# Another order of the weight units in the expert steps of a two-layer transformer trunk

## The reference, cut to what matters

```python
combine = jnp.sum(jax.nn.one_hot(top_idx, 8) * top_w[..., None], axis=1)
for e in range(8):
    out = out + combine[:, e:e+1] * ((silu(t @ w_gate[e]) * (t @ w_up[e])) @ w_down[e])
```

## Time and profile before

| | us |
|---|---|
| median of 3 runs | 1396.77 (1396.05 to 1397.29) |
| the profiled execution, its own time | 1399.85 |
| its span from the first to the last instruction | 1398.1 |
| expert units on TensorE, from the first to the last | 505.19 to 1379.86 |
| TensorE matmul busy, share of the span | 1339.7 (96%) |
| VectorE busy | 1245.5 (89%) |
| ScalarE busy | 957.7 (68%) |
| DMA moved | 467.14 MB, mean 334 GB/s |

### The profile page before, as it was taken

The page is one execution under the profiler, slowest core; times in us unless marked ns, Lnnn a source line. Parts: engine busy times, 40 slices in busy tenths (PEclk is TensorE's granted clock), DMA queues, the critical chain, the costliest instruction groups (busy, mean ns, idle before and its releaser), DMA issues.

```text
span 1398.1 us, 17800 instructions
## 1 busy us (share of the span) xinstructions
PE 1339.7 (96%) x6825; PEld 1109.5 (79%) x6825; DVE 1245.5 (89%) x1070; ACT 957.7 (68%) x899; POOL 136.1 (10%) x134
## 2 busy tenths in 40 slices
PE   4999899999999899999999999999999999999995
PEld 4868799998877787877788878788877788887774
DVE  6888998887757679999989999999999998999996
ACT  5455443333545568788778797878787887888884
POOL 4099100000048000000000000000000000000000
PEclk9999999999899979999999999999999999999998
DMA  9970799986662249999999999999999999999992
GB/s 357 384 251 31 286 334 327 336 302 212 214 215 92 101 170 410 405 398 415 399 411 384 382 411 413 408 406 399 371 405 413 407 406 408 372 392 415 412 402 113
DMA packets 140434, 467.14 MB, mean 334 GB/s; under 512 B 8734, under 2 KB 10940, under 8 KB 126012
## 3 DMA queue, kind: packets, MB, share of 16 engines
q1 hardware_dynamic: 139856, 465.90, 86.9%
q10 hardware_dynamic: 492, 0.08, 0.0%
HBM read 464.90 MB, written 1.05 MB: 333 GB/s over the span
## 4 chain that ended last, share of the span: by engine, by line
PE 70%; DVE 23%; ACT 3%; issue 2%; DMA 2%; DVEq 0%; SPq 0%; ACTq 0%
PE bank L1865 17%; PE bank L1866 16%; PE bank L1867 16%; DVE w_lo L1483 8%; PE bank L2337 3%; PE bank L2336 3%; DVE more_lo L1483 3%; DVE fifth_lo L1483 3%; DVE ring_sum L1216 1%; PE bank L2395 1%; PE bank L2397 1%; DVE w_lo L1127 1%; PE bank L2273 1%; PE bank L1891 1%; PE bank L2282 1%
## 5 line engine op out<-in xcount | busy, mean ns | idle before, releaser
L1483 DVE TENSOR_TENSOR w_lo<-raw,w_hi 128x2048 fp32r<-128x2048 f32 x202 | 455.5, 2283 | 23.1 <-ACT w_hi L693 23.0
L693 ACT ACTIVATE w_hi<-raw 128x2048 fp32r<-128x2048 f32 x202 | 384.5, 1919 | 70.7 <-PE bank L1867 53.7
L669 ACT ACTIVATE w_hi<-raw 128x2048 fp32r<-128x2048 f32 (+1 forms) x54 | 102.2, 1894 | 116.5 <-PE bank L1867 96.5
L1483 DVE TENSOR_TENSOR fifth_lo<-raw,fifth_hi 128x2048 fp32r<-128x2048 f32 x67 | 153.0, 2283 | 7.4 <-ACT fifth_hi L693 7.4
L1483 DVE TENSOR_TENSOR more_lo<-raw,more_hi 128x2048 fp32r<-128x2048 f32 x67 | 153.0, 2283 | 5.4 <-ACT more_hi L693 5.3
L1127 DVE TENSOR_TENSOR w_lo<-raw,w_hi 128x2048 fp32r<-128x2048 f32 (+1 forms) x54 | 123.3, 2287 | 24.4 <-ACT w_hi L669 24.2
L693 ACT ACTIVATE fifth_hi<-raw 128x2048 fp32r<-128x2048 f32 x67 | 128.6, 1919 | 24.0 <-PE bank L1867 17.4
L693 ACT ACTIVATE more_hi<-raw 128x2048 fp32r<-128x2048 f32 x67 | 128.6, 1919 | 18.2 <-PE bank L1867 13.6
L1865 PE MATMUL bank<-h_hi,w_hi 128*128 128x256 f32 x448 | 128.4, 287 | 0.9 <-DVE gate_m L1194 0.8
L1866 PE MATMUL bank<-h_lo,w_hi 128*128 128x256 f32 x448 | 126.7, 283 | 0.0
L1867 PE MATMUL bank<-h_hi,w_lo 128*128 128x256 f32 x448 | 126.7, 283 | 0.0
(11 more groups left out here) (375 smaller groups left out, 2905.6 us busy)
## 6 DMA issues: line engine op xcount, KB each, us to landing
raw<-in_w_ex_gate SPq DMA_DIRECT2D x112, 1024.0 KB, 9.1
raw<-in_w_ex_up SPq DMA_DIRECT2D x112, 1024.0 KB, 9.7
raw<-in_w_ex_down SPq DMA_DIRECT2D x112, 1024.0 KB, 9.9
raw<-in_w_ada SPq DMA_DIRECT2D x48, 1024.0 KB, 7.4
raw<-in_w_in SPq DMA_DIRECT2D x12, 1024.0 KB, 9.7
raw<-in_w_ff_gate SPq DMA_DIRECT2D x10, 1024.0 KB, 7.4
raw<-in_w_ff_up SPq DMA_DIRECT2D x10, 1024.0 KB, 6.5
raw<-in_w_ff_down SPq DMA_DIRECT2D x10, 1024.0 KB, 6.0
```

The costliest lines, as they stand in the source:

```text
L669: act_e.activation(w_hi[:, s % SPLIT, 0:words], raw[:, n % RAW, 0:words], ACT.Copy).then_inc(hi_done, 1)
L693: act_e.activation(dst, raw[:, (N0 + n) % RAW, :], ACT.Copy).then_inc(hi_done, 1)
L1483: dve.tensor_tensor(lo, raw[:, (N0 + n) % RAW, :], hi.bitcast(F32), ALU.subtract).then_inc(lo_done, 1)
```

## The change

The order becomes Wg Nd Wu Ng Wd Nu in steps 0 to 2, and Wg Wu Nd Ng Nu Wd stays in step 3. The work is the same; every copy, sum and transpose gets a new place. `turn_l` goes to the middle of Ng in steps 0 to 2, into banks 2 and 3 in all of them, `add_up` from the wide down to after the first Wg unit of the next step, and `turn_s` from after the first to after the second Wg unit. `scatter` goes from behind Ng into Wu, between its third and fourth unit. On VectorE `gated_l` now stands behind the third Ng unit, `low_l` behind the second Wd unit, `gated_s` behind the third Wg unit (in step 3 behind the first Wu), `low_s` behind the second Nd unit, `narrow_low_rows` behind the first Ng unit and `gate_row` 0 and 1 behind the fourth.

```diff
             if s > 0:
-                o += [(p, "S", "down", s - 1, i) for i in range(2 * len(TOGETHER[s - 1]))]
-            elif p > 0:
-                o += [(p - 1, "S", "down", FINAL, i) for i in range(2)]
-            o += [(p, "S", kind, s, i) for kind in ("gate", "up") for i in range(n)]
-            o += [(p, "L", "down", s, i) for i in range(n)]
...
+            if s < FINAL:
+                o += step("L", "gate") + downs + step("L", "up") + step("S", "gate") + step("L", "down") + step("S", "up")
+            else:
+                o += step("L", "gate") + step("L", "up") + downs + step("S", "gate") + step("S", "up") + step("L", "down")
...
     def turned_l(p, s, a):
-        return 6 + a if (p, s) == (0, 0) else 3 if s == FINAL else 2 + a
+        return 3 if s == FINAL else 2 + a
```

ScalarE:

```diff
+                    if key == ("S", "down") and i == 1 and u not in last_downs:
+                        high_s(q, s)
+                    if u == (p, "L", "up", 0, 2) and p > 0:
+                        silu_l(0, 0)
+                        silu_l(0, 1)
+                    if mine and key == ("L", "up") and i == 0 and 0 < s < FINAL:
+                        silu_l(s, 0)
+                        silu_l(s, 1)
...
-                    if mine and s < FINAL and (key, i) == ((("S", "gate"), 3) if s > 0 else (("S", "up"), 0 if p > 0 else 3)):
+                    if mine and key == ("L", "down") and i == 1 and s < FINAL:
                         high_l(s, 0)
                         high_l(s, 1)
...
-                    if mine and key == ("S", "up") and i == 3:
+                    if mine and key == ("L", "down") and i == 3:
                         keep_gate(s, 0)
                         keep_gate(s, 1)
...
+                    if mine and s > 0 and (key, i) == ((("L", "gate"), 3) if s < FINAL else (("L", "up"), 1)):
+                        keep_up(p, s - 1, 0)
+                        keep_up(p, s - 1, 1)
...
-                    if u == (p, "S", "gate", 0, 3) and p > 0:
+                    if u == (p, "S", "gate", 0, 0) and p > 0:
                         narrow_rows(p - 1)
```

VectorE:

```diff
+                    if key == ("S", "down") and i == 1 and u not in last_downs:
+                        low_s(q, s)
+                    if mine and key == ("S", "gate") and i == 2:
+                        gated_l(s, 0)
+                        gated_l(s, 1)
...
+                    if mine and key == ("L", "down") and i == 1 and s < FINAL:
                         low_l(s, 0)
                         low_l(s, 1)
...
-                    if mine and key == ("L", "gate") and i == 1 and s > 0:
+                    if mine and s > 0 and (key, i) == ((("L", "gate"), 2) if s < FINAL else (("L", "up"), 0)):
                         gated_s(p, s - 1)
...
+                    if u == (p, "S", "gate", 0, 0) and p > 0:
+                        narrow_low_rows(p - 1)
                     if u == (p, "S", "gate", 0, 3) and p > 0:
                         gate_row(p - 1, 0)
                         gate_row(p - 1, 1)
```

TensorE:

```diff
+                        if i == 0 and s > 0:
+                            add_up(s - 1)
+                        if i == 1 and before_s > 0:
                             turn_s(*old)
...
+                    if s < FINAL and before_s > 0:
+                        narrow_downs()
...
+                    for i in range(n):
+                        into_l("up", s, i, (2, 3) if s < FINAL else (3,))
+                        if (s, i) == (0, 2) and p > 0:
+                            scatter(p - 1)
+                    if s == FINAL:
+                        narrow_downs()
...
                     for i in range(n):
                         into_s("gate", s, i, (0, 1))
+                        if i == 1 and s < FINAL:
+                            turn_l(s)
...
+                    pe.wait_ge(elo_done, p * EC + (chunks_of[-1] + 1))
...
+                    if s < FINAL:
+                        for i in range(n):
+                            into_s("up", s, i, (2, 3))
```

More of the change, by code:

```diff
@@ L217, in body_of @@
             n = 2 * len(cs)
-            o += [(p, "L", kind, s, i) for kind in ("gate", "up") for i in range(n)]
             if s > 0:
-                o += [(p, "S", "down", s - 1, i) for i in range(2 * len(TOGETHER[s - 1]))]
-            elif p > 0:
-                o += [(p - 1, "S", "down", FINAL, i) for i in range(2)]
-            o += [(p, "S", kind, s, i) for kind in ("gate", "up") for i in range(n)]
-            o += [(p, "L", "down", s, i) for i in range(n)]
+                downs = [(p, "S", "down", s - 1, i) for i in range(2 * len(TOGETHER[s - 1]))]
+            else:
+                downs = [(p - 1, "S", "down", FINAL, i) for i in range(2)] if p > 0 else []
+            step = lambda who, kind: [(p, who, kind, s, i) for i in range(n)]
+            if s < FINAL:
+                o += step("L", "gate") + downs + step("L", "up") + step("S", "gate") + step("L", "down") + step("S", "up")
+            else:
+                o += step("L", "gate") + step("L", "up") + downs + step("S", "gate") + step("S", "up") + step("L", "down")
         return o
@@ L1702, in pair @@
                         low_l(FINAL, 0)
-                    if mine and key == ("L", "gate") and i == 1 and s > 0:
+                    if mine and s > 0 and (key, i) == ((("L", "gate"), 2) if s < FINAL else (("L", "up"), 0)):
                         gated_s(p, s - 1)
-                    if u == (p, "L", "gate", 0, 3) and p > 0:
+                    if u == (p, "L", "gate", 0, 2) and p > 0:
                         gated_s(p - 1, FINAL)
@@ L1708, in pair @@
                         wide_low_rows(p - 1)
[L1709 to L1714, removed]
+                    if u == (p, "S", "gate", 0, 0) and p > 0:
+                        narrow_low_rows(p - 1)
                     if u == (p, "S", "gate", 0, 3) and p > 0:
-                        narrow_low_rows(p - 1)
-                    if u == (p, "S", "up", 0, 3) and p > 0:
                         gate_row(p - 1, 0)
                         gate_row(p - 1, 1)
[L1720 to L1729, removed]
+                    if mine and s == 0 and p > 0 and key == ("L", "down"):
+                        if i < 2:
+                            gate_row(p - 1, 2 + i)
+                        else:
+                            sum_row(p - 1, i - 2)
+                    if mine and s == 1 and p > 0 and key == ("L", "gate") and i < 2:
+                        sum_row(p - 1, 2 + i)
                     if u == (p, "S", "gate", FINAL, 1) and p + 1 < PAIRS:
@@ L2417, in pair, with narrow_downs @@
                             gather_s(0)
-                        if i == (0 if s > 0 else 1) and before_s > 0:
+                        if i == 0 and s > 0:
+                            add_up(s - 1)
+                        if i == 1 and before_s > 0:
                             turn_s(*old)
[L2421 to L2428, removed]
+                    def narrow_downs():
                         pe.wait_ge(flo_done, p * S4 + s)
@@ L2444, in pair @@
                         into_s("gate", s, i, (0, 1))
-                        if s == 0 and p > 0 and i == 1:
-                            turn_l(0)
+                        if i == 1 and s < FINAL:
+                            turn_l(s)
                         if (s, i) == (FINAL, 1) and p + 1 < PAIRS:
@@ L2474, in pair @@
                             gather_s(p + 1)
-                        if i == (0 if s == FINAL else 1):
+                        if i == 0 and s == FINAL:
                             add_up(s)
```

44 lines of the change are left out of this document (7 added, 37 removed).

## The result

The changed kernel takes 1411.13 us, the median of four executions (1408.17 to 1414.52); the kernel before took 1396.41 beside it. The ratio is 1.0103, 95% interval 1.0090 to 1.0117. The prediction said 1406.6, range 1394 to 1413: direction and place were right, and the step to find is why 14.7 us came where the sum had 9.8. The time lies above the 1403 to 1410 that was given for the likeliest case. The profiled execution took 1414.52, the longest of the four, with a span of 1412.8, again 14.7 over the one before. One of the twelve executions of a later run (`low_earlier`) took 1824.84 us at a mean granted clock of 0.678; its ratio goes by the other eleven, whose median is 1401.51.

The account below looks back on a forecast made before the run. TensorE, VectorE and DMA were taken as within a few per cent of each other; new VectorE-order loops less removed waits gave +0.4, +5.5 and +3.9, +9.8 us, hence a median of 1406.6 us, range 1394 to 1413.

Parts of the forecast that it names:

- the sum: Whole kernel: pair 0 +0.4, pairs 1 and 2 +2.7 each, pair 3 +3.9, together +9.8 us, 0.7%.
- the likeliest case: Whole kernel: the two VectorE loops bind as computed, slower, 1403 to 1410 us; chance 0.65.
- Removed waits, 10.3 us: TensorE's old waits in pair 0's step 0 and all steps 1 and 2: 0.57 + 6 x 1.36 + 2 x 0.76.
- the ruler's 58.65: TensorE's work in a step of twelve wide and twelve narrow units, turns and sums: 58.65 us without waits.
- Loop of steps 1 and 2: VectorE from `gated_s` to `low_l` takes 37.6 us against TensorE's 36.5: wait 1.15 before Wd0, 1.25 with restart.
- Step 0: Pairs 1 to 3: VectorE from `gated_l` to `low_l` takes 11.2 us against TensorE's 8.34; TensorE waits 2.86 before Wd0.
- it waits 2.86 and restarts at 0.10: 2.96, three times: TensorE before Wd0 in step 0 of pairs 1 to 3: wait plus pipeline restart, 2.96 us each.
- rival (c): Slower still: TensorE waits 2.3 us at the scatter in Wu for `ys_lo`, three times, +6.9, 1413.5 us; chance 0.11.
- Step 3: Last step of a pair keeps its order; expected to take 41.1 us.
- Rival (a): Faster: neither VectorE loop binds, waits of 10.3 us vanish, 1386.5 us; chance 0.11.
- It costs nothing as long as those 10 us are spare: ScalarE has 50 us of work in a 60 us step, so copying `turn_l`'s output after Wd1 costs nothing.
- DMA: A pair's loads need 214.3 us, under the 220.25 of now, so they hide unless a pair gets shorter.

Follow-up runs that it names:

- `low_earlier`: Changed kernel with `high_l` (ScalarE) and `low_l` (VectorE) behind the first Wd unit's instruction, not the second's; 1401.65 us, ratio 1.0027.
- the last two runs: Changed kernel with `low_l` and `gate_row` edits, plus `keep_gate` one high half earlier on ScalarE: 1400.94 us; then also `keep_up` one unit earlier: 1390.49 us.
- the last run: Changed kernel with `low_l` and `gate_row` edits, plus ScalarE's copies `keep_gate` and `keep_up` each one unit earlier; 1390.49 us, ratio 0.9954; also the fastest run.
- The operation put inside: Changed kernel plus one unread VectorE operation behind the second Wu subtraction of steps 1 and 2, eight times; 1420.29 us, ratio 1.0164.
- `after_again`: The changed kernel run once more, unchanged, as reference for the other runs; 1411.43 us, ratio 1.0101.
- Both edits: Changed kernel with `high_l`/`low_l` behind the first Wd unit, `gate_row` 0 and 1 ahead of `gated_l`, and `gate_row` 2 behind `low_l`; 1398.24 us, ratio 1.0013.
- the filled run: Changed kernel with 11 unread matmuls put into TensorE's wait for `low_l` in step 0 of pairs 1 to 3; 1408.15 us, ratio 1.0078.
- the run with `keep_gate` earlier: Changed kernel with `low_l` and `gate_row` edits, plus `keep_gate` behind the third Wd unit's high half, not the fourth's; 1400.94 us, ratio 1.0026.

## Why the prediction was right, and which term was missing

- **Removed waits, 10.3 us.** Right, and to be measured only in the last two runs: where nothing else is late, steps 1 and 2 take 58.6 to 59.0 for the ruler's 58.65, and 60.01 before. Over the eight of them in the last run, and pair 0's step 0, that is 9.5 of the 10.3.
- **Loop of steps 1 and 2.** Right: waits of 1.17 for 1.15, steps of 59.89 for 59.9. VectorE idles 0.65 and 1.86 us before `gated_s` in pair 1, as computed (0.8 and 2). The operation put inside shows that the loop is closed: 0.6 us more in it is 0.59 more wait.
- **Step 0.** The wait was right (2.88 for 2.86), and so was its cause: moving 1.2 us of `gate_row` out and 0.6 behind took 1.8 us off it.
- **Where it failed.** The step "it waits 2.86 and restarts at 0.10: 2.96, three times" priced the restart from waits of a few tenths. Behind 2.88 us the restart costs 0.10 in some places and 1.4 to 2.8 us more in others, as the clock falls to 0.50. In the profiled execution this added 4.3 us, in that of `after_again` 3.1, and with the wait filled nothing. I had looked at the clock in the windows of before, where it is 1.00, and hadn't asked what the new wait would do to it. That 1411.1 still lies within 1394 to 1413 is luck in part: the room above 1410 was there for rival (c), which didn't occur.
- **Step 3.** 41.07 for 41.1.
- **Rival (a)** gave as its condition that `low_l` is ready within 36.5 and 8.34 us. Both edits met it and gave 1398.2, not 1386.5: the condition was too weak. "It costs nothing as long as those 10 us are spare", said of ScalarE, holds only for its total; where its list puts a copy is what counts. `keep_gate` behind one high half more cost 0.6 a step, and `keep_up` behind a high half that waits for its load cost 1.1 to 4.5 us in step 3.
- **Rival (c)** didn't occur: no wait for `ys_lo` in a pair's Wu. **DMA** was no bound for the changed kernel: its share is 0.95 in step 0, and where it is 1.03, in step 2, the step takes the 59.9 of the loop. In the fastest run ScalarE waits for loads from step 1 on, yet TensorE doesn't until the last step.

Open: why the clock falls behind some of the 2.9 us waits and not behind others, and where the last 0.8 us or so of the filled run's 11.2 come from.

## What to carry to other kernels

Price a reordering by its loops: from the instruction at which an in-order engine must stop for TensorE, through its list, to the one for which TensorE stops, against TensorE's own work in between. A wait that a loop adds may cost more than its length, as the clock can fall behind it; work that nobody needs, put into the wait, took that back, and moving a small operation out of the loop is better. When one loop is opened, look for the small copies that its wait had covered, and for what the edit itself put ahead of them on the other engine. Move them ahead of the long operations, those that wait for loads above all, and all together: with the copies left where they were, two opened loops brought nothing over the kernel before; with the copies moved too, it was 0.5%.

## What was not expected of the hardware

- Behind a wait of 2.88 us the granted clock fell to 0.50 in nine of twelve places (four profiled executions with that wait unfilled: 2, 2, 3 and 2 of 3), and behind the waits of 1.1 to 1.8 us, and one of 2.12, in none. A fall cost 1.4 to 2.8 us.
- In the run with `keep_gate` earlier it fell behind the waits of 2.9, 2.75 and 2.4 us at `add_up` and not behind the one of 2.16.
- With eleven matmuls whose result nobody reads in each of the three waits, the clock stayed at 1.00 and the kernel took 3.3 us less.
